# Row chains by banks, an output product by tiles, and norm weights behind the transposes, in one kernel

## The reference

```python
def first_block(x, ...):
    for l in range(DEPTH):                                   # DEPTH = 2
        y = mixer(x, w_in[l], ..., w_o[l], cos, sin)         # three attention branches, gates, then merged @ w_o
        x = layer_norm(DN_ALPHA * x + y, ln1_g[l], ln1_b[l])
        y = moe(x, router_w, router_b, moe_w_gate, ...)      # 16 experts in 4 groups, a token goes to 2 of one group
        x = layer_norm(DN_ALPHA * x + y, ln2_g[l], ln2_b[l]) # (x - mean) * rsqrt(var + eps) * g + b
    return x

def second_block(x, norm_pre, norm_post, ...):
    for l in range(DEPTH):
        h = rms_norm(x, norm_pre[l, 0])
        x = x + 0.5 * rms_norm(swiglu_ffn(h, ...), norm_post[l, 0])
        h = rms_norm(x, norm_pre[l, 1])
        x = x + rms_norm(hybrid_mixer(h, ...), norm_post[l, 1])      # ends in merged @ w_out
        h = rms_norm(x, norm_pre[l, 2])
        x = x + 0.5 * rms_norm(swiglu_ffn(h, ...), norm_post[l, 2])
    return x
```

## Time and profile before

| | |
|---|---|
| runs | 2381.06, 2383.14, 2383.84 us; median 2383.14 |
| profiled execution | 2383.86 us |
| its span in the trace | 2382.3 us |
| mean granted TensorE clock | 0.994 |
| busy: TensorE, VectorE, ScalarE, GpSimd | 96%, 74%, 59%, 10% |
| moved | 497.33 MB, mean 209 GB/s |

### The profile page before, as it was taken

The page is one execution under the profiler, slowest core; times in us unless marked ns, Lnnn a source line. Parts: engine busy times, 40 slices in busy tenths (PEclk is TensorE's granted clock), DMA queues, the critical chain, the costliest instruction groups (busy, mean ns, idle before and its releaser), DMA issues.

```text
span 2382.3 us, 39448 instructions
## 1 busy us (share of the span) xinstructions
PE 2298.4 (96%) x11114; PEld 1875.9 (79%) x11114; DVE 1755.2 (74%) x2348; ACT 1409.6 (59%) x1892; POOL 236.9 (10%) x296
## 2 busy tenths in 40 slices
PE   9998999999998999999999999999999999989998
PEld 7777788878777788877887867888878877778887
DVE  6778888887778888897556788765565568887555
ACT  5653777774653777774446576454464466765445
POOL 0000000000000000000000692000000008800000
PEclk9999999999999999999999999999999999999999
DMA  7444899985444799995555544565656554455652
GB/s 263 129 144 133 303 340 332 345 326 160 151 135 152 277 336 335 342 333 191 185 185 177 163 140 150 186 205 185 193 188 186 184 179 141 156 170 161 211 184 97
DMA packets 277777, 497.33 MB, mean 209 GB/s; under 512 B 20512, under 2 KB 112848, under 8 KB 277632
## 3 DMA queue, kind: packets, MB, share of 16 engines
q1 hardware_dynamic: 273440, 481.60, 60.6%
q0 software_dynamic: 4192, 14.02, 2.0%
HBM read 494.50 MB, written 1.05 MB: 208 GB/s over the span
## 4 chain that ended last, share of the span: by engine, by line
PE 69%; DVE 14%; DVEq 6%; issue 4%; ACT 3%; DMA 1%; ACTq 1%; PEldq 0%; SPq 0%; PEld 0%; POOLq 0%
PE g_bank L625 14%; PE g_bank L626 13%; PE g_bank L627 13%; PE s_bank L627 8%; PE s_bank L625 8%; PE s_bank L626 8%; DVE w_lo L598 4%; DVE conv_y L2700 2%; DVEq L2694 1%; PE t_bank L1783 1%; DVEq L2304 1%; ACT w_hi L593 1%; PE t_bank L1943 1%; DVE row_max L2328 1%; PE t_bank L1807 0%
## 5 line engine op out<-in xcount | busy, mean ns | idle before, releaser
L598 DVE TENSOR_TENSOR w_lo<-w_raw,w_hi 128x1024 fp32r<-128x1024 f32 x909 | 1095.7, 1235 | 337.0 <-ACT w_hi L593 312.2
L593 ACT ACTIVATE w_hi<-w_raw 128x1024 fp32r<-128x1024 f32 x909 | 944.5, 1058 | 408.1 <-PE g_bank L627 170.3
L625 PE MATMUL g_bank<-w_hi,xt_hi 128*128 128x512 f32 (+1 forms) x1136 | 453.8, 399 | 11.5 <-ACT gate L1401 5.1
L626 PE MATMUL g_bank<-w_lo,xt_hi 128*128 128x512 f32 (+1 forms) x1136 | 442.6, 390 | 0.0
L627 PE MATMUL g_bank<-w_hi,xt_lo 128*128 128x512 f32 (+1 forms) x1136 | 442.4, 389 | 0.0
L625 PEld LDWEIGHTS g_bank<-w_hi,xt_hi 128*128 128x128 f32 x1136 | 215.6, 190 | 67.0 <-issue 13.4
L627 PEld LDWEIGHTS g_bank<-w_hi,xt_lo 128*128 128x128 f32 x1136 | 215.2, 189 | 45.3
L626 PEld LDWEIGHTS g_bank<-w_lo,xt_hi 128*128 128x128 f32 x1136 | 215.6, 190 | 40.3
L625 PE MATMUL s_bank<-w_hi,xt_hi 128*128 128x512 f32 x608 | 240.2, 395 | 0.0
L627 PE MATMUL s_bank<-w_hi,xt_lo 128*128 128x512 f32 x608 | 237.3, 390 | 0.0
L626 PE MATMUL s_bank<-w_lo,xt_hi 128*128 128x512 f32 x608 | 236.9, 390 | 0.0
(11 more groups left out here) (366 smaller groups left out, 2887.2 us busy)
## 6 DMA issues: line engine op xcount, KB each, us to landing
w_raw<-in_w_in_dram SPq DMA_DIRECT2D x192, 512.0 KB, 4.6
w_raw<-in_moe_w_gate_dram SPq DMA_DIRECT2D x128, 512.0 KB, 5.3
w_raw<-in_moe_w_up_dram SPq DMA_DIRECT2D x128, 512.0 KB, 5.6
w_raw<-in_moe_w_down_dram SPq DMA_DIRECT2D x128, 512.0 KB, 5.3
w_raw<-in_ffn_w_gate_dram SPq DMA_DIRECT2D x176, 256.0 KB, 2.9
w_raw<-in_ffn_w_up_dram SPq DMA_DIRECT2D x176, 256.0 KB, 3.1
w_raw<-in_ffn_w_down_dram SPq DMA_DIRECT2D x88, 512.0 KB, 3.4
w_raw<-in_w_branch_dram SPq DMA_DIRECT2D x40, 512.0 KB, 4.4
```

Of the source, the lines that this page charges most:

```text
L593: nc.scalar.activation(half_of(w_hi, u, h), half_of(w_raw, u, h), ACT.Copy).then_inc(hi_ready, 1)
L598: nc.vector.tensor_tensor(half_of(w_lo, u, h), half_of(w_raw, u, h), half_of(w_hi, u, h).bitcast(F32), ALU.subtract).then_inc(lo_ready, 1)
L625: nc.tensor.matmul(dst, a_hi, b_hi, start=first, stop=False)
L626: nc.tensor.matmul(dst, a_hi, b_lo, start=False, stop=False)
```

## The change

It has three parts.

**1. First mixer's output product and router.** The product of the first half row of tile 0 is followed by tile 0's second half row, and tile 0's `x_quads` stand ahead of the last unit's tile 1. Splits of this stretch are moved: one half at each of several places, halves 2 and 3 of the first expert unit at the head of the round, half 4 behind the first gather. Fewer filler transposes. The norm's weights and bias are also loaded by columns (`gain_col`, `first_col`, 1024 numbers each, one run of 4 bytes a number), from POOL; VectorE waits for them before the rounds.

**2. Return.** The 32 matmuls bring tile 0 back first. VectorE makes tile 0's mean and variance inside the round. `normed` writes only (acc - mean) * root in place; TensorE transposes that; ScalarE applies weight and bias behind the transposes, where they are one number a partition (`affine`, four instructions of 128 columns a quad), then copies to `xt_hi`; VectorE subtracts (`affine_lo`). Splits of the next halves are set between these. The rows x themselves get weight and bias in eight full-width VectorE instructions at the end. Filler transposes go from 54, 8 and 64 to 12, 16 and 12 + 16.

**3. Row chains by banks.** The last down unit is multiplied half row by half row (`down_end`) and releases each bank on its own; ScalarE squares each bank as it is released (`square`), at the second mixer's end too; in `row_returned`, `scaled(1)` moves behind the first half row's steps.

```diff
         pool.dma_start(gains[:, i, :], d[w][bass.ds(l, 1), :].to_broadcast([P, DM])).then_inc(gains_in, 16)
+        pool.dma_start(gain_col[:, i, :], d[w][bass.ds(l, 1), :].rearrange("a (k p) -> p (a k)", p=P), allow_slow_non_contiguous=True).then_inc(gains_in, 16)
     if stacks == 2 and l == DEPTH - 1:
-        pool.dma_start(first_gain[:, :], d["norm_pre_2"][0:1, 0, :].to_broadcast([P, DM])).then_inc(pre_in, 16)
+        pool.dma_start(first_col[:, :], d["norm_pre_2"][0:1, 0, :].rearrange("a (k p) -> p (a k)", p=P), allow_slow_non_contiguous=True).then_inc(pre_in, 16)
...
-        for place in held:
-            ahead(place)
+            if what == "gather" and part == "start":
+                split_hi(at_r["u"], 4)
+        if held:
+            split_hi(held[0], AHEAD)
+    for h in range(2, 4):
+        split_hi(at_r["u"], h)
     all_parts(act, run)
...
-    ahead(u + 27)
-    split_hi(u + 28, AHEAD)
+    split_hi(u + 29, 1)
     for tt in range(TT):
         tile_root(tt, At(tt, (l, 4)))
+        if tt == 0:
+            split_hi(u + 30, 0)
         act_xt(t + (T_AFTER_MIX1 + 4 + 2 * tt), 2, TILE[tt])
     act.preload_act_table_set("sigmoid_and_others")
-    for h in range(2, 4):
-        split_hi(u + 30, h)
+    split_hi(u + 30, 1)
     act.wait_ge(s_ready, (at["s"] + (S_LAYER - 1)).value(1, 1))
     act.activation(router_t[:, :], s_bank[0:NE, 0:TT * P], ACT.Sigmoid).then_inc(s_free, 1)
     act.drain().then_inc(router_t_ready, 1)
-    split_hi(u + 30, 4)
...
+        tf = t_next + (2 * tt + kq)
+        act.wait_ge(t_ready, tf.value(1, 1))
+        for j in range(4):
+            k = 4 * kq + j
+            last = act.activation(xt_full[:, tt, kq, j * P:(j + 1) * P], t_bank[tf.slot(2)][:, j * P:(j + 1) * P], ACT.Identity,
+                                  scale=gain_col[:, 0, k:k + 1], bias=gain_col[:, 1, k:k + 1])
+        last.then_inc(t_free[tf.slot(2)], 1)
+        act.drain()
+        act.activation(xt_hi[:, 4 * kq:4 * kq + 4, tt * P:(tt + 1) * P],
+                       xt_full[:, tt, kq, :].rearrange("p (a b) -> p a b", a=4), ACT.Copy).then_inc(xt_hi_ready, 1)
+    act.activation(root_of[:, :], c("ones", 0, 1), ACT.Sqrt)
+    act.wait_ge(first_var_ready, done)
+    act.activation(rstd[:, 0:1], rstd[:, 0:1], ACT.Sqrt).then_inc(rstd_ready, 1)
+    act.wait_ge(cols_ready, l + 1)
+    affine(0, 0)
+    tile_root(1, At(3, (l, 4)))
+    split_hi(u_next, 2)
+    affine(0, 1)
+    split_hi(u_next, 3)
+    affine(1, 0)
+    affine(1, 1)
+    split_hi(u_next, 4)
 if stacks < 2:
...
-        squares(0, fills, ffn_junk[:, :], 0.5)
+        for nb in range(2):
+            act.wait_ge(out_ready, out_at(l, i) + nb + 1)
+            square(0, nb, fills, ffn_junk[:, :], 0.5)
...
             act_xt(t_next, 2, [(0, 0), (0, 1)])
         split_hi(end, 3)
+        act.wait_ge(out_ready, out_at(l, i) + 3)
+        square(1, 0, fills, ffn_junk[:, :], 0.5)
...
     pe.wait_ge(xt_ready, 10 * l + 8)
     out_unit(1, 0, (0,)).then_inc(wo_ready, 1)
     out_unit(1, 1, (0,)).then_inc(wo_ready, 1)
+    out_unit(0, 1, (1,))
     out_unit(1, 0, (1,))
+    x_quads(t + (T_AFTER_MIX1 + 4), 8 * l + 4, 0)
     out_unit(1, 1, (1,))
     pe.wait_ge(router_split, 2)
     spare = in_round(l, done)["g"]
     for tt in range(TT):
         if tt:
             idle_products(g_wait(spare), 20)
-        x_quads(t + (T_AFTER_MIX1 + 4), 8 * l + 4, tt)
-        if tt:
-            idle_products(g_wait(spare), 11)
+            x_quads(t + (T_AFTER_MIX1 + 4), 8 * l + 4, tt)
...
-        for groups in (range(NG - 1), (NG - 1,)):
+        for tt, groups in ((0, range(NG - 1)), (0, (NG - 1,)), (1, range(NG - 1)), (1, (NG - 1,))):
             pe.wait_ge(y_ready, 4 * rnd + (groups[-1] + 1))
-            for i in range(4):
...
+            if tt == 0:
+                pe.wait_ge(tile_t_ready, 2 * l + (w + 1))
+            else:
+                pe.wait_ge(ffn_t_ready, q10.value(1, 1))
+            part = slice(tt * P, (tt + 1) * P)
+            for nb in range(2):
+                for k in range(2):
+                    half_is_split(d10, k)
+                    c0 = k * DM + nb * 512
+                    last = mm3(g_bank[(f + (4 + 2 * tt + nb)).slot(4)][:, :], ffn_t_hi[:, 1, k, part], ffn_t_lo[:, 1, k, part],
+                               w_end_hi[:, c0:c0 + 512], w_end_lo[:, c0:c0 + 512], False, k == 1)
+                if tt and nb:
+                    last.then_inc(w_used, 2)
...
+        if tt == 0:
+            split_lo(u + 30, 0)
     dve.drain().then_inc(x_ready, 1)
     dve_xt(t + (T_AFTER_MIX1 + 6), At(14, (l, 16)), 2, TILE[1])
-    for h in range(2, 4):
-        split_lo(u + 30, h)
+    split_lo(u + 30, 1)
...
+    def variance(tt):
+        dve.drain()
+        dve.bn_aggr(mean_var[:, tt, :], stats[:, tt, :])
+        dve.drain()
+        dve.tensor_scalar(mean_var[:, tt, 1:2], mean_var[:, tt, 1:2], LN_EPS, None, ALU.add)
+        dve.drain()
+        return dve.reciprocal(rstd[:, tt:tt + 1], mean_var[:, tt, 1:2])
...
+    dve.wait_ge(gains_in, 96 * l + 96)
+    if l == DEPTH - 1 and stacks == 2:
+        dve.wait_ge(pre_in, 16)
+        dve.tensor_tensor(gain_col[:, :, :], gain_col[:, :, :], first_col[:, :].unsqueeze(1).to_broadcast([P, 2, 8]), ALU.mult)
+    dve.drain().then_inc(cols_ready, 1)
...
+            if i == 1:
+                variance(0).then_inc(first_var_ready, 1)
         dve.drain()
     dve.reg_add(rho, rho, R)
...
     done = dve.snap(rho, min_val=0, max_val=4)
     gain, bias = gains[:, 0, :], gains[:, 1, :]
     if l < DEPTH - 1:
-        t_next, n_next = layer1(l + 1, done)["t"], At(0, (l + 1, 16))
+        u_next, n_next, row_sem = layer1(l + 1, done)["u"], At(0, (l + 1, 16)), row_ready
     elif stacks == 2:
-        t_next, n_next = layer2(0, done)[0]["t"], At(16 * DEPTH)
+        u_next, n_next, row_sem = layer2(0, done)[0]["u"], At(16 * DEPTH), normed_ready
+    def normed(tt):
+        dve.drain()
+        dve.wait_ge(rstd_ready, At(2 + tt, (l, 4)).value(1, 1))
+        for kq in range(2):
+            a_ = acc[:, tt, kq * 512:(kq + 1) * 512]
+            dve.tensor_scalar(a_, a_, mean_var[:, tt, 0:1], rstd[:, tt:tt + 1], ALU.subtract, ALU.mult).then_inc(row_sem, 1)
+    def affine_lo(tt, kq):
+        dve.wait_ge(xt_hi_ready, (n_next + (2 * tt + kq)).value(1, 1))
+        part = slice(tt * P, (tt + 1) * P)
+        dve.tensor_tensor(xt_lo[:, 4 * kq:4 * kq + 4, part], xt_full[:, tt, kq, :].rearrange("p (a b) -> p a b", a=4),
+                          xt_hi[:, 4 * kq:4 * kq + 4, part].bitcast(F32), ALU.subtract)
+        dve.drain().then_inc(xt_ready, 1)
+    dve.sem_inc(var_ready, 1)
+    normed(0)
+    for nb in range(2):
+        row_stats(acc, 1, nb)
+    variance(1).then_inc(var_ready, 1)
+    affine_lo(0, 0)
+    normed(1)
+    split_lo(u_next, 2)
+    affine_lo(0, 1)
+    split_lo(u_next, 3)
+    affine_lo(1, 0)
+    affine_lo(1, 1)
+    split_lo(u_next, 4)
     for tt in range(TT):
-        for nb in range(2):
-            row_stats(acc, tt, nb)
-        if tt and (stacks == 2 or l < DEPTH - 1):
-            dve_xt(t_next, n_next, 2, TILE[0], each=True)
-        norm_first(acc, x, tt, gain, 64 * l + 64)
-        for kq in range(2):
-            norm_second(x, tt, At(2 + tt, (l, 4)), bias, (kq,))
-            if l == DEPTH - 1 and stacks == 2:
-                norm_in(ffn_y, 0, 0, tt, kq, first_gain)
-        if tt:
-            dve.drain().then_inc(x_ready, 1)
-    if stacks == 2 or l < DEPTH - 1:
-        dve_xt(t_next + 2, n_next + 2, 2, TILE[1], each=True)
+        for gain_row, op in ((gain, ALU.mult), (bias, ALU.add)):
+            dve.drain()
+            for kq in range(2):
+                cols = slice(kq * 512, (kq + 1) * 512)
+                dve.tensor_tensor(x[:, tt, cols], (acc if op == ALU.mult else x)[:, tt, cols], gain_row[:, cols], op)
+    dve.drain().then_inc(x_ready, 1)
...
         dve.wait_ge(square_ready, 15 * l + (sq + 2 * tt + 1))
         scaled(0)
+        dve.drain()
         dve.wait_ge(square_ready, 15 * l + (sq + 2 * tt + 2))
         dve.scalar_tensor_tensor(out=rstd[:, tt:tt + 1], in0=mean_sq[:, tt, 0:1], scalar=RMS_EPS * (times / factor) ** 2,
                                  in1=mean_sq[:, tt, 1:2], op0=ALU.add, op1=ALU.add)
         dve.drain()
         dve.reciprocal(rstd[:, tt:tt + 1], rstd[:, tt:tt + 1]).then_inc(var_ready, 1)
-        scaled(1)
-        dve.drain()
         dve.wait_ge(rstd_ready, At(8 + n + tt, (l, 11)).value(1, 1))
         for nb in range(2):
+            if nb:
+                scaled(1)
+                dve.drain()
             cols = slice(nb * 512, (nb + 1) * 512)
             dve.scalar_tensor_tensor(out=x[:, tt, cols], in0=dst[:, tt, cols], scalar=rstd[:, tt:tt + 1], in1=x[:, tt, cols],
                                      op0=ALU.mult, op1=ALU.add)
```

100 lines of the change are left out of this document (54 added, 46 removed).

## The result

The changed kernel takes 2386.27 us (median of 19 runs, 2383.32 to 2389.54), the kernel before 2381.31 (19 runs, 2378.97 to 2383.84). The ratio is 1.0021, with a 95% interval of 1.0015 to 1.0027: slower by 3.6 to 6.4 us. The forecast was 0.15% slower, with a range that holds 2386.27.

A forecast was written before the change was run, and what follows sets the result against it. TensorE, busy 96% of the span, was taken as the bound, time leaving only through its idle stretches and fillers. Terms -4.0, +0.8, +4.85, +2.35, less 0.3, gave +3.7: 2386.8 us as a median, range 2376 to 2392.

The forecast's parts named there:

- Part 1, layer 0: First mixer's output product and router: first expert product at 238.9 instead of 240.90, 2.0 us gained.
- Part 1, layer 1: The same stage in the second layer: the same gain of 2.0 us, 4.0 in all for both layers.
- The column loads: Loads `gain_col` and `first_col` before each round: landed by 231 to 232, VectorE asks at 233.7, costed at nothing.
- Rival C: Before the round: column loads not there when asked, 3.5 us lost twice, 2393.8 us; chance 0.12.
- The return, layer 0: Experts' return: first product 4.0 us earlier, but half 5 split late, so TensorE goes on 0.8 us later.
- The return, layer 1: Return before the feed-forward block: early start lost in a 7 us wait, hidden tile transposed 4.85 us later.
- rival D: At the return: a table reload before each `affine`, adding 7.7 us, 2394.5 us; chance 0.04.
- Rival B: At the return: half 5 there when TensorE asks, gains of 1.5 and 4.4 us kept, 2375.6 us; chance 0.20.
- Part 3: Row chains by banks: second half row 0.57 us later at three feed-forward ends; 2.35 us later in sum.
- The 0.1 at the second mixers: Ends of the second mixer: first square goes ahead, saves 0.6 and gives it back, 0.1 us later each.
- Rival E: Row chains: the bank-wise chains win through early first squares, 1.5 us gained, 2383 us; chance 0.04.
- the 0.3 for filled bank waits: Smaller bank waits that the reordering may fill in part: 0.3 us off the sum, +4.0 to +3.7.

The follow-up runs named there:

- part 1 alone: Only the first mixer's output product by tiles with its moved splits, applied to the kernel before: ratio 0.9989 to the kernel before.
- gap_filled: The changed kernel with 16 filler transposes in TensorE's gap before the first expert product: ratio 1.0008 to the kernel before.
- scaled_back: The changed kernel with `scaled(1)` put back behind the reciprocal: ratio 1.0006 to the kernel before.
- half5_first: The changed kernel with half 5 of the next stage split before the eight instructions that write x: ratio 1.0016 to the kernel before.
- x_between: The changed kernel with x written in VectorE's idle time between quads, half 5 split behind half 4, first silu ahead of three splits: ratio 0.9967 to before.
- best_of_all: The changed kernel with x written between the quads, the gap before the first expert product filled, `scaled(1)` back: 2369.84 us, 0.9952 to the kernel before.
- part 3 alone: Only the row chains by banks, applied to the kernel before: ratio 1.0013 to the kernel before.

## Why the prediction was right

The change is slower by 5.0 us where 3.7 were forecast, and for the reasons given; one term was wrong. That the median of 2386.27 lies only 0.5 from the 2386.8 forecast is luck: the forecast stood on a median of before of 2383.14 from three runs, 1.8 above that of nineteen, and the difference was 1.3 too small; the two errors cancel.

- **Part 1, layer 0.** Quads forecast at 212.46 came at 213.17, and the first expert product at 239.34 where 238.9 stood. The trace of after began 0.65 us late (product 6), which explains most of both. Term -2.0, measured -2.2; alone -2.4. In the trace of after all of it is kept; in the trace of part 1 alone the clock fell behind the first expert product and took 1.55 of it, which the term doesn't have either.
- **Part 1, layer 1: the term that was wrong.** I took layer 0's 2.0 for it, and the changed kernel has -0.2. The start of the experts did come 1.8 us earlier, but TensorE stood 2.62 us before it, its clock fell to 0.50, and 1.56 us went. The step that failed is the price of the gap: it was put at its own length, and the clock behind it at nothing. I had read the wait of 1.64 in the earlier trace rows, added to it the two splits' shift, and not asked what the longer gap does to the clock. `gap_filled` shows the cause: with TensorE busy in the gap the clock stays at 1.00 and the 1.56 come back.
- **The column loads.** They landed 4.6 to 5.9 us after their issue, as the router's weights did (5.5), and VectorE never waited for a load there. Rival C falls. Whether each number is a descriptor of its own, as the rule cited says (the Trainium skill, DMA: Bandwidth & Descriptors, Rules for kernel authors), these times can't tell: 4 KB in 1024 runs took 4.6 to 5.9 us, the router's 64 KB in 1024 runs 5.3, and GpSimd's broadcast loads of 512 KB 4.0 to 6.3 in the same trace. So neither the bytes nor the runs show in the time to landing at these sizes.
- **The return, layer 0.** First product 3.8 earlier (forecast 4.0), `normed` 0.543 us (0.55), four instructions of `affine` 1.51 (1.7), x written for 5.4 (5.6), wait for half 5 2.04 (2.35 by the forecast's times). Term +0.8, measured +0.5 with the clock at 1.00 behind the wait. In the three traces where it was 0.50 there the stretch is 2.0 over before, outside the term's bound of 1.5: the term has the wait and not the clock behind it.
- **The return, layer 1.** Wait of 6.85 where 7 stood. Term +4.85, measured +4.5. I had called the low clock behind the wait hidden; it was there, 0.50 until 1118, and set the pace of the products from 1300 to 1304. Nearly all of it was hidden: the hidden tile was ready at 1117.4 and transposed at 1118.06, and in the four other kernels with this wait the clock rose earlier, TensorE waited for the tile (0.45 in `scaled_back`) and the four products took 5.18 to 5.19 instead of 5.77. `half5_first` shows that the root of the next norm would have held TensorE as long: two things were late by the same cause, x.
- **No table load** stands before Identity; rival D falls. The trace agrees with the rule cited (the Trainium skill, ScalarE: Activation LUTs, Table sets: the hidden batching unit; identity is in every set) that such a load isn't needed.
- **Rival B** (half 5 ready when asked) would have needed the eight instructions somewhere else. `x_between` puts them there, and what B counted on is then real: 67.24 and 42.56 in `best_of_all` are 2.0 and 4.7 under before, where B had 1.5 and 4.4.
- **Part 3.** Forecast 0.57 at each of three ends; measured 0.59, 0.60 and 0.57, and 0.5 at the very end. The 0.1 at the second mixers doesn't show (19.45 from 1848 to 1872, 19.50 before; 20.22 and 20.21 from 2712 to 2740). Rival E, by which the chains by banks win, falls with part 3 alone (1.0013 [1.0004, 1.0022]).
- **The sum.** The terms gave +3.7 from -4.0, +0.8, +4.85, +2.35 and -0.3; measured are -2.4, +0.5, +4.5 and +2.3. The miss of 1.6 in part 1 is larger than the 1.3 between forecast and runs; the return was forecast 0.65 too dear, and the 0.3 for filled bank waits did not come. These are the sizes in one pair of traces; the low clock in layer 0 could have added about 1.5 at each of two places.

## What to carry to other kernels

When a chain is shortened at its front, ask what has been moved to its end and who reads that: here x and the next split came last, and a lead of 5.6 us in layer 1 was paid back in one wait. Instructions that nobody waits for now but somebody will soon belong into the idle time between hand-overs, on the engine that is idle in any case; the cover of a short round trip to another engine (`scaled(1)` behind the reciprocal) is worth its own length. And a longer gap on TensorE is costed with the clock behind it, as a chance: here 1.5 to 1.6 us each time that it fell, in some traces of the same wait and not in others.
